# Moving the rotation of the attention's queries and keys from VectorE to Pool in the two third-kind mixers

## The reference, cut to what matters

```python
z = h @ w_in[l]                      # 1024 -> 8704 columns
zq, zf, zi, zg, zatt, za, zb = split(z)
o_hg = gated linear recurrence of zq, zf, zi, gated by zg
qkv = zatt.reshape(B, S, 3, N_GROUPS, ATT_HEADS, ATT_DIM)   # 3 groups, 4 heads of 128
for g, (window, dilation) in enumerate(ATT_GROUPS):
    qg = partial_rope(qkv[:, :, 0, g], cos, sin)
    kg = partial_rope(qkv[:, :, 1, g], cos, sin)
    ... dilated window attention of qg, kg, vg ...

def partial_rope(t, cos, sin):       # the first 32 of 128 dimensions
    r1, r2 = t[..., :16], t[..., 16:32]
    return concatenate([r1 * cos - r2 * sin, r2 * cos + r1 * sin, t[..., 32:]])
```

## Time and profile before

| | us |
|---|---|
| median of 3 runs | 1879.49 (1879.48 to 1879.52) |
| the profiled execution | 1879.31 |
| its span, first to last instruction | 1877.5 |
| PE busy | 1863.6 (99%) |
| DVE busy | 1265.3 (67%) |
| ACT busy | 944.4 (50%) |
| POOL busy | 62.9 (3%) |

### The profile page before, as it was taken

How to read it: one execution, slowest core, us unless ns; L and a number is a source line. 1 busy time by engine, 2 the same in 40 slices (tenths; PEclk the granted TensorE clock), 3 DMA queues, 4 the chain that set the end, 5 groups by cost and what they waited for, 6 DMA issues and landing times.

```text
span 1877.5 us, 25275 instructions
## 1 busy us (share of the span) xinstructions
PE 1863.6 (99%) x9637; PEld 1586.2 (84%) x9637; DVE 1265.3 (67%) x1559; ACT 944.4 (50%) x1225; POOL 62.9 (3%) x94
## 2 busy tenths in 40 slices
PE   9999999999999999999999999999999999999998
PEld 7888988888888898888889888888889888888886
DVE  4466786466546668745576997677656797776754
ACT  5454574554345446445446545545444645445543
POOL 1010100000000000000000000000000000000000
PEclk9999999999999999999999999999999999999999
DMA  9667545656665665666555554455665554465562
GB/s 327 193 195 218 196 140 193 192 181 186 207 195 183 180 187 145 207 198 184 181 173 185 164 181 143 134 193 186 201 192 174 181 191 159 133 190 170 189 191 79
DMA packets 173656, 342.58 MB, mean 182 GB/s; under 512 B 10992, under 2 KB 11168, under 8 KB 173424
## 3 DMA queue, kind: packets, MB, share of 16 engines
q1 hardware_dynamic: 169376, 327.26, 56.1%
q0 software_dynamic: 4176, 13.90, 2.3%
HBM read 338.49 MB, written 1.05 MB: 181 GB/s over the span
## 4 chain that ended last, share of the span: by engine, by line
PE 88%; DVE 10%; issue 1%; ACT 1%; POOL 0%; POOLq 0%; DVEq 0%; ACTq 0%
PE stream L2365 18%; PE stream L2367 18%; PE stream L2366 18%; PE stream L2560 6%; PE stream L2561 3%; PE aux L2418 3%; DVE wlo L1313 3%; PE stream L2540 3%; PE stream L2541 3%; PE stream L2542 3%; PE stream L2403 2%; PE stream L2394 1%; PE stream L2395 1%; PE stream L2477 1%; PE stream L2479 1%; PE stream L2478 1%
## 5 line engine op out<-in xcount | busy, mean ns | idle before, releaser
L1313 DVE TENSOR_TENSOR wlo<-raw,whi 128x1024 fp32r<-128x1024 f32 x582 | 703.8, 1222 | 472.2 <-ACT whi L786 469.3
L786 ACT ACTIVATE whi<-raw 128x1024 fp32r<-128x1024 f32 x582 | 607.1, 1056 | 543.6 <-PE stream L2367 429.6
L2365 PE MATMUL stream<-whi,x_split 128*128 128x512 f32 x944 | 373.3, 395 | 1.5 <-DVE ak L1324 0.6
L2367 PE MATMUL stream<-whi,x_split 128*128 128x512 f32 x944 | 368.1, 390 | 0.0
L2366 PE MATMUL stream<-wlo,x_split 128*128 128x512 f32 x944 | 367.5, 389 | 0.0
L2365 PE MATMUL stream<-whi,hhi 128*128 128x512 f32 x672 | 263.3, 392 | 0.0
L2367 PE MATMUL stream<-whi,hlo 128*128 128x512 f32 x672 | 261.6, 389 | 0.0
L2366 PE MATMUL stream<-wlo,hhi 128*128 128x512 f32 x672 | 261.5, 389 | 0.0
L2560 PE MATMUL stream<-x_split,whi 128*128 128x512 f32 x672 | 241.4, 398 | 2.8 <-DVE ak L1324 2.1
L2367 PEld LDWEIGHTS stream<-whi,x_split 128*128 128x128 f32 x944 | 177.2, 188 | 37.9
L2365 PEld LDWEIGHTS stream<-whi,x_split 128*128 128x128 f32 x944 | 177.3, 188 | 37.3 <-DVE x_split L1349 1.5
(11 more groups left out here) (345 smaller groups left out, 2105.9 us busy)
## 6 DMA issues: line engine op xcount, KB each, us to landing
raw<-ffn_w_gu SPq DMA_DIRECT2D x175, 512.0 KB, 4.4
raw<-w_in SPq DMA_DIRECT2D x136, 512.0 KB, 4.6
raw<-ffn_w_down SPq DMA_DIRECT2D x88, 512.0 KB, 3.8
raw<-w_up SPq DMA_DIRECT2D x64, 512.0 KB, 4.4
raw<-w_down SPq DMA_DIRECT2D x64, 512.0 KB, 4.3
raw<-c_w_in SPq DMA_DIRECT2D x24, 512.0 KB, 3.9
raw<-ab_w_in SPq DMA_DIRECT2D x20, 512.0 KB, 4.9
raw<-w_out SPq DMA_DIRECT2D x16, 512.0 KB, 3.7
```

What stands on the lines that cost most here:

```text
L786: act.activation(split_slots(lin, at, j)[0], raw[:, b % RAW], ACT.Copy).then_inc(hi_ready, 1)
L1313: dve.tensor_tensor(lo, raw[:, b % RAW], hi.bitcast(F32), ALU.subtract).then_inc(lo_ready, 1)
L2365: pe.matmul(bank[tt][:], hi, wh, start=kt == 0, stop=False)
L2367: mm = pe.matmul(bank[tt][:], lo, wh, start=False, stop=kt == last)
```

## The change

Pool now does the three instructions of each rotation itself, right behind the two transfers that it issues for them and a wait for their landing. A new semaphore `turned_half` stands between the two products and the sum. VectorE's `use(c)` no longer has the rotation. The semaphore `roped` is now counted by Pool; who waits for it is as before.

```diff
--- before.py
+++ after.py
@@ -502,6 +502,7 @@
         param_in = sem("param_in")
         side_in = sem("side_in")
         roped = sem("roped")
+        turned_half = sem("turned_half")
 
         swap_in = [sem(f"swap_in{i}") for i in range(2)]
         logits_ready = sem("logits_ready")
@@ -718,6 +719,7 @@
 
             def swaps(st):
 
+                pool.wait_ge(const_in, 32)
                 for c in range(5, 11):
                     tiles = (aq if c < 8 else ak)[:, 4 * ((c - 5) % 3):4 * ((c - 5) % 3) + 4]
 
@@ -726,8 +728,17 @@
 
                         pool.wait_ge(roped, seen.roped - 1 + seen.rotated)
                     seen.roped += 1
+                    other, part = rope_swap[c % 2], tiles[0:32]
                     for to, half in ((0, 16), (16, 0)):
-                        pool.dma_start(rope_swap[c % 2][to:to + 16], tiles[half:half + 16]).then_inc(swap_in[c % 2], 16)
+                        pool.dma_start(other[to:to + 16], tiles[half:half + 16]).then_inc(swap_in[c % 2], 16)
+                    seen.swaps += 1
+
+                    pool.wait_ge(swap_in[c % 2], 32 * ((seen.swaps + 1) // 2))
+                    table = lambda name: cst(name, 32).unsqueeze(1).to_broadcast([32, 4, S])
+                    pool.tensor_tensor(other[:], other[:], table("sin_b"), ALU.mult).then_inc(turned_half, 1)
+                    pool.tensor_tensor(part, part, table("cos_b"), ALU.mult).then_inc(turned_half, 1)
+                    pool.wait_ge(turned_half, 2 * seen.swaps)
+                    pool.tensor_tensor(part, part, other[:], ALU.add).then_inc(roped, 1)
 
             for n, st in enumerate(stages):
                 side(st)
@@ -2161,18 +2172,6 @@
                         decay_pairs(c - 3)
                     if 3 <= c <= 10:
                         decay_to(c - 2)
-                    if 5 <= c <= 10:
-                        group = (c - 5) % 3
-                        part = (aq if c < 8 else ak)[0:32, 4 * group:4 * group + 4]
-                        other = rope_swap[c % 2]
-                        seen.swaps += 1
-
-                        dve.wait_ge(swap_in[c % 2], 32 * ((seen.swaps + 1) // 2))
-                        shape = [32, 4, S]
-                        step(dve.tensor_tensor(other[:], other[:], over(cst("sin_b", 32), shape), ALU.mult))
-                        step(dve.tensor_tensor(part, part, over(cst("cos_b", 32), shape), ALU.mult))
-                        dve.tensor_tensor(part, part, other[:], ALU.add).then_inc(roped, 1)
-                        seen.roped += 1
                     if c == 13:
                         head_copies()
```

## The result

| | before | after |
|---|---|---|
| median of the runs | 1879.49 us | 1920.43 us (1918.82 to 1922.29) |
| ratio to before, 95% interval | | 1.0218 (1.0203 to 1.0234) |
| span of the profiled execution | 1877.5 us | 1917.0 us |
| mean granted clock of TensorE | 0.999 | 0.992 |
| VectorE instructions, busy | 1559, 1265.3 us | 1523, 1282.6 us |

The forecast was 1892 us, in a range of 1874 to 1903 us. The sign was right, the size was not: +40.9 us in place of +12.4.

A forecast was written before the change was run, and what follows sets the result against it. PE bounds the kernel, but VectorE sets the pace by a little at chunk ends. Holds by Pool cost (4 x 1.8 - 1.0) x 2 = 12.4 us: 1879.49 + 12.4 = 1891.9, so 1892 us, range 1874 to 1903 us.

The forecast's parts named there:

- the first two tiles at 0.8 us: Chunks 5 and 6 of each mixer: chunk 5 free, chunk 6 costing 1.8 us less 1.0 us in hand.
- VectorE sets the pace, by a little: Chunk 8: VectorE busy 12.60 of 12.70 us, PE alone 12.2; PE's waits of 4.9 us could come back.
- VectorE then stands for ScalarE for 2.1 us: Each chunk without rotation on VectorE: it waits from 1070.6 to 1072.7 for the exponential and the rounded block.
- Pool's instruction takes 2.25 us: Each of Pool's three 1024-element instructions for a tile: 2.25 us, bounds 0.91 and 3.2 us.
- Pool's reads deny VectorE the shared path, for whole instructions: VectorE instructions with two SBUF inputs wait while Pool streams its inputs; assumed, as only the other direction was shown.
- Holds of 3.3 us in a chunk: Three Pool instructions hold VectorE 0.15, 2.25 and 0.9 us: chunk 14.5 us against 12.70, 1.8 us more.
- rival "strict turns": Two Pool instructions fall before the pause, one into it: 4.7 us of holds, +23 us, 1902 us; chance 0.11, with longer instructions.
- At the first I take off 1.0 us, because VectorE comes into chunk 6 with time in hand: Chunk 6 of each mixer: 1.0 us less cost, since VectorE stood for 2.07 us in chunk 5.
- the swaps of chunks 4 and 9 ... cost nothing: First and last tiles of each mixer: no cost, since PE doesn't wait for additions there.
- Pool is in time: Pool needs 6.75 us for a tile, under a chunk; last tiles have 18.7 us before roped is wanted: no cost.
- 6.2 forecast: Cost for one mixer: four chunk ends, chunks 6 to 9, at 1.8 us each, less 1.0 us at the first.

The follow-up runs named there:

- experiment 1: Changed kernel without Pool's three rotation instructions; transfers and counts of roped stay, nobody rotates: 1872.86 us, ratio 0.9965 to the kernel before.
- experiments 2 and 3: Changed kernel, Pool's three rotation instructions replaced for each tile by nine memsets (1872.94 us) or by five one-input copies (1889.24 us); rotation not computed.
- experiment 5: Changed kernel, but Pool's first rotation instruction waits until decay_to of that chunk is done, to start in VectorE's pause: 1907.19 us, ratio 1.0148.
- experiment 8: Changed kernel with only the first two of six rotations of a mixer on Pool, the other four on VectorE: 1899.91 us, ratio 1.0105.
- experiment 6: Changed kernel with PE doing each level's matmuls four times for levels 2 to 5, to keep its clock up: 1923.50 us, ratio 1.0237.
- experiment 11: Kernel before with each swap sent as eight transfers in place of two, 96 in place of 24, nothing else: 1885.20 us, ratio 1.0032.

## Why the prediction was wrong, point by point

The mechanism was right. What failed is where the holds fall: the forecast put Pool's first instruction into VectorE's pause, and took the first two tiles at 0.8 us and the last at nothing for each mixer. They cost 9.0 and 1.5 us in the first mixer.

- *VectorE sets the pace, by a little*: right. Each added microsecond on VectorE was paid by PE, and without the rotation the time fell (experiment 1). Its gain was 6.6 us, not 4.9.
- *VectorE then stands for ScalarE for 2.1 us*: right, 2.07 us wherever the pause shows.
- *Pool's instruction takes 2.25 us*: 2.39 us free, inside the bounds of 0.91 and 3.2 us, and up to 3.3 us where VectorE holds it. The Trainium skill, GPSIMD Engine Reference, section 3.1, had given the same 2.25 us as an estimate, 6% below the trace.
- *Pool's reads deny VectorE the shared path, for whole instructions*: right, and shown from both sides (experiments 2 and 3). The rule of the Trainium skill, SBUF — State Buffer, section "Who interferes with whom", agrees with this trace in both directions (2.90 us for 0.69 on VectorE, 2.83 for 2.40 on Pool).
- *Holds of 3.3 us in a chunk*: mis-sized. The walk put Pool's first instruction into the pause. It starts when its data land, which is while VectorE is at the short products of `decay_to`. By turns, each of these waits for a whole instruction of Pool, however short it is itself. In chunk 8 two of the three fall there, 2.2 + 2.2 us, and the third into the pause: 12.70 - 3.63 + 2.07 + 4.4 = 15.5 us for chunk 8; the additions are 15.71 us apart. That is the walk of the rival "strict turns", whose chunk would be 12.70 + 3.1 = 15.8 us; I gave it 0.11. When Pool was moved into the pause (experiment 5), the forecast's own 14.5 us came out, as 14.68. So the price of a hold was right, and the place was read wrong, though the prediction's own text had Pool's data landing at 1069.4, ahead of the pause. Cost: three chunks x (3.0 - 1.8) = 3.6 us for each mixer.
- *"At the first I take off 1.0 us, because VectorE comes into chunk 6 with time in hand", and "the swaps of chunks 4 and 9 ... cost nothing"*: this is the step that failed most. The first tile's first instruction started at 1033.94, beside the `wlo` pair at 1033.96, which took 6.75 us for 2.36, and the third lay over the next pair (3.27 us). That PE didn't wait for VectorE there before was no cover against 4.4 us of holds. In chunk 6 Pool starts as long after the additions as in chunk 8 (5.4 and 5.5 us), but VectorE comes to its products 1.5 us later, by the 0.91 us of the held pair and by a COPY_PREDICATED of 128x512 that takes 1.34 us for 0.76. So Pool's instructions meet three short products in a row: chunk 6 is 14.44 - 3.63 - 0.94 (two waits of VectorE for ScalarE that are gone) + 2.07 + 0.91 (the second `wlo` pair) + 6.21 (the three products) = 19.06 us, measured 18.97. Chunks 5 and 6 cost 9.0 us, and 9.3 in the second mixer, against 0.8: 8.2 us missed in the first. Experiment 8 has it alone, 9.2 us.
- The last tile, the swap of chunk 9, was priced at nothing too. It holds the two `decay_to` instructions of chunk 10 (the first 2.62 us, at the end of this document), and the stretch of chunks 10 to 12 is 1.5 us longer. PE didn't wait for VectorE there before; now VectorE, without its 3.63 us but with the pause and two holds, is late with the next `wlo`, for which PE stands 0.24 us in the first mixer and 1.74 us in the second (experiment 6).
- The sum for the first mixer: 6.2 forecast + 8.2 + 3.6 + 1.5 = 19.5 us, as measured.
- *Pool is in time*: right. PE waits nowhere for `roped`.
- The range ended at the strict turns, whose sum made the same assumptions on the first and the last tiles, so it shared the step that failed.

## What to carry to other kernels

A transfer of work to Pool is not free even if Pool is idle: while Pool reads SBUF, each VectorE instruction that has both inputs in SBUF waits for one of Pool's (a copy out of SBUF did too, additions with one input in PSUM did not), so the cost is the number of such instructions met times Pool's instruction time, whatever their own length. Walk it from the time at which Pool's data land, at every tile and not at the one in the middle, and take the cover of a stage only after the holds are put in. Expect that number to change with the moment at which Pool starts: it was one to three in a chunk here. First look whether the instruction is wasteful where it is: an instruction on 32 of 128 partitions was made 3.3 times shorter on VectorE by transfers, and this version is faster than both kernels.

## What the runs showed of the hardware that was not expected

- A copy on VectorE with one input in SBUF is held like a product: 2.62 us, where the same shape takes 0.42 in the kernel before (a product of this shape takes 0.69). VectorE after, chunk 10:

```profile
1112.82 2.62 DVE L2046 COPY decayed<-decay_sum 128x512 f32<-128x512 f32 x1
```

and before:

```profile
1094.80 0.42 DVE L2035 COPY decayed<-decay_sum 128x512 f32<-128x512 f32 x1
```

- The hold doesn't depend on VectorE's length: 0.42 us became 2.61 and 0.69 became 2.89. It is there though Pool works on 32 partitions and VectorE on 128, and though the tiles are different ones.
- Memsets on Pool, 8.9 us for a tile, held nothing.
- The program's end waited for PE's queue by 1.3 us before and 7.0 us in experiment 11, with the work of the engines up to there no later. Its cause wasn't found.
